# One joined first stage, and experts in 32-row blocks on four column groups with a fixed order of weights

## The chip, the cores and the metric

The kernel runs on one core of one Trainium2 chip. The metric is the device time of one execution in microseconds (us). The core has five engines with a queue of instructions each: TensorE (PE) for products and transposes, VectorE (DVE), ScalarE (ACT), GpSimd (POOL) and SyncE (SP). They meet through semaphores. SP, POOL and ACT issue transfers, which 16 DMA engines carry out.

## The reference, cut to what matters

Two streams, 256 context rows and 1024 latent rows of D = 1024, pass a convolution layer and a gated linear attention (GLA) layer. Each layer is followed by a mixture of 32 experts, in which every row goes to two experts of one group. All data are float32. The first layer works on all 1280 rows, the second one on the 1024 latent rows.

```python
x = x + sincos_2d(...)                         # latent rows only
h = modulate(rmsnorm(x, g), shift, scale)      # h * (1 + scale) + shift, from silu(c) @ ada_w + ada_b
a, g = split(h @ pw1_w + pw1_b); u = depthwise_conv31(a * sigmoid(g))   # then layernorm, silu, pw2
# experts: top-1 of 4 groups, top-2 of its 8 experts; for each pair of row and expert e
y = (silu(h @ w1[e]) * (h @ w3[e])) @ w2[e]    # 1024 -> 512 -> 1024, weighted sum of two
```

With the reference's inputs the router gives each expert of layer 0 between 1 and 14 blocks of 32 rows, 96 in all (42 blocks of 128 rows); in the fixed order of the change they are 1, 2, 1, 12, 1, 1, 1, 8, 3, 1, 1, 6, 1, 2, 1, 8, 2, 1, 1, 11, 4, 1, 1, 2, 1, 1, 1, 3, 1, 1, 1, 14. Layer 1 has 79 blocks of 32 rows (32 of 128): one expert with 1, sixteen with 2, fourteen with 3, one with 4. Every expert has at least one block, used or not.

## The kernel before, in words

The program is a row of stages with a barrier between them. Tiles have 128 rows: 2 of context, 8 of latent rows.

`modulation` computes the shift and scale rows of layer 0 (4 loads of 2 MB of `ada_w`, `ada_acc`) and adds the position to the latent rows on DVE (L191). `normalise` loads the rows back, scales them (L295, L298), transposes them on TensorE into `norm_pt` and writes the high part (ACT, L263) and the low part (DVE, L302) of the transposed rows, `ht_conv_hi` and `ht_conv_lo`. `conv_taps` then loads the first columns of the weights, splits them too (L516, L555), and computes product, gate (L563) and the 31 taps, channels of 128 at a time; the taps run on DVE. Next to it, modulation rows of later stages are computed as units of four column groups of TensorE (L488, `taps_ada_acc`).

The function `product3` (L97 to L101) is the float32 product of the expert stage: with each operand split in a high and a low part it issues three fast products, high by high (L99), low by high (L100), high by low (L101).

`route` plans a layer's blocks: DVE picks the experts and counts ranks, two small products give sums, DVE builds two tables, and 20 products `route_pi` (L1048) turn them into the list of rows of each block, `plan_token`. `plan_block` holds each block's expert, `plan_fresh` whether it is a new one.

`experts` walks over blocks of 128 rows in a loop whose body holds two blocks. SP reads the block's expert from `plan_block` and, where it is fresh, loads three matrices of 2 MB as six halves of 1 MB (`moe_w_raw`, L1282), each once the raw buffer has been split. ACT makes the high parts (L1408), DVE the low ones (L1479). POOL gathers the block's rows (`moe_xg`), TensorE transposes them (L1349), multiplies with the pair w1 and w3 (`moe_pg`, `moe_pu`), transposes the product (`moe_pat`, L1388) and multiplies with w2 (`moe_py`) one block late. ACT stores the result (`scratch_experts_out`). A block takes 24 calls of `product3`, that is 72 products of 128x512: 16 calls for the pair, 8 for w2. The later stages `combine_values` and `combine` gather the results by `plan_slot`.

## Time and the profile before

| what | value |
|---|---|
| median of 3 runs | 3072.42 us (3071.2 to 3075.68) |
| profiled execution | 3072.33 us, span 3070.6 us |
| mean granted clock | 0.899 |
| PE, DVE, ACT, POOL busy | 82%, 65%, 47%, 11% of the span |
| DMA | 689.13 MB, 224 GB/s over the span |

The stages by their first instruction: modulation from 0 us, `normalise` 66, `conv_taps` 120.9, `conv_out` 545, `route` 737.8, `experts` 781, `combine_values` 1577, GLA 1848, second `route` 2330, second `experts` 2370, `combine` 2985 to 3070.6. A time in the rows below is one of that span; the share of an engine over the span is a mean over stages with different limits.

### The profile page before, as it was taken

How to read it: one execution, taken by the hardware profiler on the slowest of the kernel's cores; microseconds unless marked ns; L12 is line 12 of the kernel's file. 1: busy time of each engine (PE TensorE's matmuls, PEld its weight loads, DVE VectorE, ACT ScalarE, POOL GpSimd, SP SyncE). 2: the span in 40 equal slices, each digit the busy share in tenths (PEclk: the TensorE clock that was granted, in tenths of full speed). 3: DMA queues.
4: the chain of work that ended last, by engine and by line, in shares of the span. 5: the costliest groups of instructions: out<-in, count | busy, mean ns of one | idle time of the engine just before them, and what ended most of it. 6: DMA issues, size and time to landing. Idle time of an engine off the chain costs nothing. (4 is left out here: it accounts for less than half of the span.)

```text
span 3070.6 us, 40694 instructions
## 1 busy us (share of the span) xinstructions
PE 2519.3 (82%) x13249; PEld 2033.0 (66%) x13249; DVE 2006.1 (65%) x1989; ACT 1432.9 (47%) x1596; POOL 331.4 (11%) x381
## 2 busy tenths in 40 slices
PE   4488773695799999999948998979693999999970
PEld 0467662584588888888836876768583788888850
DVE  1559999665657786588526402347565788888855
ACT  0311001452546676577424313458331777777742
POOL 0000000100001000100012100043100100010004
PEclk8589887797799999999978999989796999999985
DMA  9354341221878899799655411025551999999956
GB/s 306 119 166 140 127 159 70 99 103 65 291 261 306 323 331 357 264 360 389 247 182 202 143 52 46 14 78 171 205 191 61 375 389 385 389 388 394 394 211 227
DMA packets 294341, 689.13 MB, mean 224 GB/s; under 512 B 22764, under 2 KB 49588, under 8 KB 294222
## 3 DMA queue, kind: packets, MB, share of 16 engines
q1 hardware_dynamic: 263058, 584.81, 52.8%
q0 software_dynamic: 17472, 56.72, 5.6%
q10 hardware_dynamic: 13712, 46.30, 4.0%
q8 instruction: 61, 1.00, 0.1%
q14 instruction: 38, 0.31, 0.0%
HBM read 597.74 MB, written 91.06 MB: 224 GB/s over the span
## 5 line engine op out<-in xcount | busy, mean ns | idle before, releaser
L1479 DVE TENSOR_TENSOR moe_w_lo<-moe_w_raw,moe_w_hi 128x2048 fp32r<-128x2048 f32 x384 | 861.8, 2285 | 81.8 <-ACT moe_w_hi L1408 48.0
L1408 ACT ACTIVATE moe_w_hi<-moe_w_raw 128x2048 fp32r<-128x2048 f32 x384 | 713.8, 1908 | 59.1 <-issue 38.3
L99 PE MATMUL moe_pg<-moe_w_hi,moe_xt_hi 128*128 128x512 f32 x592 | 243.4, 411 | 11.3 <-DVE moe_xt_lo L1490 5.9
L99 PE MATMUL moe_py<-moe_w_hi,moe_at_hi 128*128 128x512 f32 x592 | 242.0, 409 | 11.9 <-DVE moe_w_lo L1479 8.2
L100 PE MATMUL moe_pg<-moe_w_lo,moe_xt_hi 128*128 128x512 f32 x592 | 236.6, 400 | 0.0
L101 PE MATMUL moe_pg<-moe_w_hi,moe_xt_lo 128*128 128x512 f32 x592 | 236.1, 399 | 0.0
L100 PE MATMUL moe_py<-moe_w_lo,moe_at_hi 128*128 128x512 f32 x592 | 235.4, 398 | 0.0
L101 PE MATMUL moe_py<-moe_w_hi,moe_at_lo 128*128 128x512 f32 x592 | 235.3, 397 | 0.0
L101 PE MATMUL moe_pu<-moe_w_hi,moe_xt_lo 128*128 128x512 f32 x592 | 234.3, 396 | 0.0
L99 PE MATMUL moe_pu<-moe_w_hi,moe_xt_hi 128*128 128x512 f32 x592 | 234.1, 396 | 0.0
L100 PE MATMUL moe_pu<-moe_w_lo,moe_xt_hi 128*128 128x512 f32 x592 | 234.1, 396 | 0.0
L1525 DVE TENSOR_TENSOR moe_a<-moe_sil,moe_pu 128x512 f32<-128x512 f32 x74 | 50.9, 688 | 182.0 <-issue 133.2
L531 ACT ACTIVATE taps_sg<-taps_zg,channel_vectors 128x512 f32<-128x512 f32 (+1 forms) x24 | 14.8, 616 | 285.5 <-PE taps_za L101 285.5
L1418 ACT ACTIVATE moe_y<-moe_py 128x1024 f32<-128x1024 f32 x74 | 76.0, 1027 | 148.8 <-PE moe_py L101 148.8
L1433 ACT ACTIVATE moe_xt_hi<-moe_pxt 128x1024 fp32r<-128x1024 f32 x74 | 75.8, 1025 | 134.5 <-PE moe_pxt L1349 134.5
L99 PEld LDWEIGHTS moe_pg<-moe_w_hi,moe_xt_hi 128*128 128x128 f32 x592 | 113.1, 191 | 36.2 <-issue 12.4
L99 PEld LDWEIGHTS moe_py<-moe_w_hi,moe_at_hi 128*128 128x128 f32 x592 | 112.4, 190 | 35.9 <-issue 12.3
L1311 POOL COPY moe_idx<-plan_token 128x1 int32 (+1 forms) x76 | 16.0, 210 | 1077.1 <-PE moe_pxt L1349 1076.9
L101 PEld LDWEIGHTS moe_pg<-moe_w_hi,moe_xt_lo 128*128 128x128 f32 x592 | 113.0, 191 | 27.4
L101 PEld LDWEIGHTS moe_py<-moe_w_hi,moe_at_lo 128*128 128x128 f32 x592 | 112.2, 190 | 27.1
L99 PE MATMUL cv_acc<-cv_w_hi,ht_next_hi 128*128 128x512 f32 x288 | 116.9, 406 | 14.8 <-DVE ht_next_lo L2038 14.8
L99 PEld LDWEIGHTS moe_pu<-moe_w_hi,moe_xt_hi 128*128 128x128 f32 x592 | 111.2, 188 | 26.9
(348 smaller groups left out, 5397.5 us busy)
## 6 DMA issues: line engine op xcount, KB each, us to landing
moe_w_raw<-in_moe_w SPq DMA_DIRECT2D x384, 1024.0 KB, 12.7
taps_ada_w<-in_ada_w SPq DMA_DIRECT2D x40, 1024.0 KB, 6.9
scratch_experts_out<-moe_y ACTq DMA_DIRECT2D x57, 512.0 KB, 6.4
taps_raw<-in_conv_pw_w SPq DMA_DIRECT2D x20, 512.0 KB, 8.6
scan_v<-scratch_gla_values SPq DMA_DIRECT2D x20, 512.0 KB, 3.6
ada_w<-in_ada_w SPq DMA_DIRECT2D x4, 2048.0 KB, 29.8
cv_raw<-in_gla_w_in SPq DMA_DIRECT2D x16, 512.0 KB, 4.8
scratch_gla_out<-scan_o SPq DMA_DIRECT2D x16, 512.0 KB, 6.4
```

The lines of the kernel that those rows point to most:

```text
L99: pe.matmul(out, xh, wh, start=start, stop=False)
L100: pe.matmul(out, xh, wl, start=False, stop=False)
L101: return pe.matmul(out, xl, wh, start=False, stop=stop)
L531: act.activation(sg[g][:, 0:m], zg[g][:, 0:m], ACT.Sigmoid, bias=vecs[:, n, V_BG:V_BG + 1])\
L1311: pool.tensor_copy(idx[:, :], plan.token[:, ds(k, 1)]).then_inc(s("idx_ready"), 1)
L1408: act.activation(hi[m][:, cut, :], raw[m][p][:, cut, :], ACT.Copy).then_inc(s(f"{m}_hi{h}"), 1)
L1418: act.activation(y[:, :], py[:, :], ACT.Copy).then_inc(s("y_out"), 1)
L1433: act.activation(xt_hi[:, :, :], pxt[:, :, :], ACT.Copy).then_inc(s("xt_hi"), 1)
L1479: dve.tensor_tensor(lo[m][:, cut, :], raw[m][p][:, cut, :], hi[m][:, cut, :].bitcast(F32), ALU.subtract).then_inc(s(f"{m}_lo{h}"), 1)
L1525: dve.tensor_tensor(a[:, :], sil[:, :], pu[:, :], ALU.mult).then_inc(s("a_ready"), 1)
```

## The change

It has three parts.

1. `modulation` and `normalise` become one stage, `front`. POOL loads the rows into eight buffers; the position's row half comes from a product on TensorE (`front_pp`); ACT scales the rows by their norm, TensorE transposes them at once, and DVE copies them unmodulated into `taps_out` (`vt`). The shift and scale rows are computed as four units of four column groups, transposed, and become columns (`mod`). `conv_taps` starts by modulating the transposed rows with these columns and splitting them. The first two pieces of its weights are loaded by `front`, its small rows too. The zeros that the expert stage wrote for unused blocks (`moe_zero`) are written once, by one transfer from ACT in `conv_taps`.
2. `route` plans blocks of 32 rows. Numbers of blocks come from three operations that round (`whole`). The table of a block's expert is gone; `plan_ends` says at which block each expert ends. `route_pi` works in four column groups. The comparing row of numbers is loaded a stage earlier (`ranks`). SP issues the weights of the first three experts at once.
3. `experts` takes the experts in a fixed order, `EXPERT_ORDER`, through four buffers of 6.29 MB (`Feed`). SP loads expert x + 3 when TensorE is through with x - 1. There is no splitting: products are plain float32. A block has 32 rows and is computed in four column groups: 32 products of 32x256 for the pair (each column group another quarter of the columns), 2 transposes of x, 16 products for w2, 1 transpose. Rows come as 128 quarters of 1 KB, by gathers issued four blocks ahead. TensorE's program holds, for each expert of a body of four, four straight copies of a block's instructions and two more inside loops; a copy has some 200 instructions, TensorE's program grows from 59 to 134.6 stretches of 256 instructions.

Its core:

```diff
-GROUPS, PER_GROUP, EXPERTS, FF, BLK = 4, 8, 32, 512, 128
+GROUPS, PER_GROUP, EXPERTS, FF, BLK = 4, 8, 32, 512, 32
+EXPERT_ORDER = [g * PER_GROUP + e for e in range(PER_GROUP) for g in range(GROUPS)]
...
+                        act.activation(ht.hi[:, k, t0:t0 + m], vt[:, k, t0:t0 + m], ACT.Copy).then_inc(s("ht_hi"), 1)
...
+                def modulate(g, k):
+                    t0, m, _ = CONV_GROUPS[g]
+                    st = CTX if g == 0 else LAT
+                    dve.tensor_scalar(vt[:, k, t0:t0 + m], vt[:, k, t0:t0 + m], mod[:, SC1, st, k:k + 1],
+                                      mod[:, SH1, st, k:k + 1], ALU.mult, ALU.add).then_inc(s("modulated"), 1)
+                def row_low(g, k):
+                    t0, m, _ = CONV_GROUPS[g]
+                    dve.wait_ge(s("ht_hi"), g * KC + k + 1)
+                    dve.tensor_tensor(ht.lo[:, k, t0:t0 + m], vt[:, k, t0:t0 + m], ht.hi[:, k, t0:t0 + m].bitcast(F32),
+                                      ALU.subtract).then_inc(s("ht_lo"), 1)
+                order = [(g, k) for g in range(len(CONV_GROUPS)) for k in range(KC)]
+                LAG = 3
+                for i in range(len(order) + LAG):
+                    if i < len(order):
+                        modulate(*order[i])
+                    if i >= LAG:
...
+    BUFS, AHEAD = 4, 3
+    PAIR = 2 * KC * FF
+    WORDS = PAIR + FF // P * D
...
+    def load_pair(self, sp, x):
+        e, b = EXPERT_ORDER[x], x % self.BUFS
+        for m, src in enumerate((self.d.w1, self.d.w3)):
+            for h in range(2):
+                sp.dma_start(self.pair[:, b, m, h * KC // 2:(h + 1) * KC // 2, :].rearrange("p (s c) n -> p s (c n)", c=2),
+                             src[self.layer, e, h * D // 2:(h + 1) * D // 2, :].rearrange("(s p c) n -> p s (c n)", p=P, c=2))\
+                    .then_inc(self.sem(f"pair_loaded{b}"), 16)
+    def load_back(self, sp, x):
+        e, b = EXPERT_ORDER[x], x % self.BUFS
+        for h in range(2):
+            sp.dma_start(self.back[:, b, 2 * h:2 * h + 2, :],
+                         self.d.w2[self.layer, e, h * FF // 2:(h + 1) * FF // 2, :].rearrange("(k p) n -> p k n", p=P))\
+                .then_inc(self.sem(f"back_loaded{b}"), 16)
...
+def route(nc, d, layer, streams, plan, lg, ranks, feed):
...
-        in_blk = ph.sb("in_blk", [P, 2 * nt, nb + 1])
...
+                for x in range(feed.AHEAD):
+                    feed.load_pair(sp, x)
+                    feed.load_back(sp, x)
...
+                    if j % nt == 0:
+                        pe.wait_ge(s("hot_slots"), 2 * (j // nt + 1))
+                    for r in range(0, P, BLK):
+                        last = pe.matmul(pi[r:r + BLK, :], in_slot[:, j, :], in_blk[:, j, :],
+                                         start=j == 0, stop=j == 2 * nt - 1)
                 last.then_inc(s("slots_done"), 1)
...
+                def whole(out, values, shift, floor):
+                    link(dve.tensor_scalar(out, values, 1.0 / BLK, shift, ALU.mult, ALU.add))
+                    link(dve.tensor_scalar(out, out, ROUND, None, ALU.add))
+                    link(dve.tensor_scalar(out, out, ROUND, floor, ALU.subtract, ALU.max))
...
+                whole(over, mine, -(BLK - 1) / (2 * BLK), 0.0)
+                link(dve.tensor_tensor(first, first, over, ALU.add))
+                link(dve.scalar_tensor_tensor(mine, over, -float(BLK), mine, ALU.mult, ALU.add))
...
+                for x in range(EXPERTS):
+                    times = x // BUFS + 1
+                    sp.wait_ge(feed.sem(f"pair_loaded{x % BUFS}"), 64 * times)
+                    sp.sem_inc(s("pair_ready"), 1)
+                    sp.wait_ge(feed.sem(f"back_loaded{x % BUFS}"), 32 * times)
+                    sp.sem_inc(s("back_ready"), 1)
+                    if 1 <= x < EXPERTS - feed.AHEAD:
+                        done = sp.value_load(plan.ends[0:1, x - 1:x], min_val=1, max_val=nb)
+                        sp.wait_ge(s("pair_done"), done)
+                        feed.load_pair(sp, x + feed.AHEAD)
+                        sp.wait_ge(s("back_done"), done)
+                        feed.load_back(sp, x + feed.AHEAD)
...
+                    pool.tensor_copy(idx[:, p:p + 1], plan.token[:, ds(k, 1)]).then_inc(s("idx_ready"), 1)
+                    pool.wait_ge(s("idx_ready"), k + 1)
                     pool.sem_inc(s("gathers"), 1)
...
+                    pool.indirect_dma_start(xg[p][:, :], None, cut_rows, bass.IndirectOffsetOnAxis(idx[:, p:p + 1], 0))\
+                        .then_inc(s(f"gathered{p}"), 16)
...
+                def out_product(out, buf):
+                    for c in range(STRIPS):
+                        for j in range(STRIPS):
+                            last = pe.matmul(out[j * BLK:(j + 1) * BLK, 0:CUT], at[:, c * BLK:(c + 1) * BLK],
+                                             feed.back[:, buf, c, j * CUT:(j + 1) * CUT], start=c == 0, stop=c == STRIPS - 1)
+                    last.then_inc(s("back_done"), 1)
+                def rows_of(k, x, b, nth):
+                    pe.wait_ge(s("xt_ready"), k + 1)
+                    if nth == 0:
+                        pe.wait_ge(s("pair_ready"), x + 1)
+                    for c in range(KC):
+                        for j in range(STRIPS):
+                            last = pe.matmul(pg[j * BLK:(j + 1) * BLK, 0:2 * P].rearrange("t (m n) -> t m n", m=2),
+                                             xt[:, c % 2, (c // 2) * BLK:(c // 2 + 1) * BLK],
+                                             feed.pair[:, b, :, c, j * P:(j + 1) * P], start=c == 0, stop=c == KC - 1)
+                    last.then_inc(s("pair_done"), 1)
+                    turn_x(k + 1)
+                    if started(k, 1):
+                        pe.wait_ge(s("at_ready"), k)
+                        if nth < 2:
+                            pe.wait_ge(s("back_ready"), x + nth)
+                        pe.wait_ge(s("y_out"), k)
+                        out_product(py, (b - 1) % BUFS if nth == 0 else b)
+                    pe.wait_ge(s("a_ready"), k + 1)
+                    pe.transpose(pat[:, 0:P], a[:, :], ident[:, :]).then_inc(s("at_turned"), 1)
+                def expert(x, b):
+                    first = 0 if isinstance(x, int) and x == 0 else \
+                        pe.value_load(plan.ends[0:1, ds(x - 1, 1)], min_val=1, max_val=nb)
+                    end = pe.value_load(plan.ends[0:1, ds(x, 1)], min_val=1, max_val=nb)
+                    rows_of(first, x, b, 0)
+                    for r in range(1, SOME):
+                        with pe.If(first + r < end):
+                            rows_of(first + r, x, b, r)
+                    with pe.If(first + SOME < end):
+                        with pe.Fori(SOME, MANY) as r:
+                            with pe.If(first + r < end):
+                                rows_of(first + r, x, b, SOME)
+                        with pe.If(first + MANY < end):
+                            with pe.Fori(MANY, (nb - EXPERTS) // 2) as r:
+                                with pe.If(first + r < end):
+                                    rows_of(first + r, x, b, SOME)
+                SOME, MANY = 4, 16
                 pe.wait_ge(s("ident"), 16)
-                turn_x(1)
-                blocks(pe, body, lambda count, last: out_product(count, last, 1))
+                turn_x(0)
+                for b in range(BUFS):
+                    expert(b, b)
+                with pe.Fori(1, EXPERTS // BUFS) as i:
+                    for b in range(BUFS):
+                        expert(i * BUFS + b, b)
+                count = pe.value_load(plan.block[0:1, 0:1], min_val=plan.fewest, max_val=nb)
+                pe.wait_ge(s("at_ready"), count)
+                pe.wait_ge(s("back_ready"), EXPERTS)
+                out_product(py_last, (EXPERTS - 1) % BUFS)
             @block.scalar
             def _(act):
                 act.preload_act_table(ACT.Silu)
```

TensorE's queue in the expert stage before: the end of one block, the branch to the loop's next block, and the start of its products.

```order
L99 MATMUL moe_py<-moe_w_hi,moe_at_hi 128x512
L100 MATMUL moe_py<-moe_w_lo,moe_at_hi 128x512
L101 MATMUL moe_py<-moe_w_hi,moe_at_lo 128x512
L1388 MATMUL moe_pat<-moe_ident,moe_a 128x128 x4
L1225 UNCONDITIONAL_BRANCH
L1225 ISA
L1228 COMPARE_AND_BRANCH
L1371 REGISTER_ALU
L99 MATMUL moe_pg<-moe_w_hi,moe_xt_hi 128x512
```

In the changed kernel TensorE has this between two experts: two values are read, then comes the first block of the expert and, behind a branch, the next.

```order
L1382 TENSOR_LOAD plan_ends
L1382 ISA x2
L1383 TENSOR_LOAD plan_ends
L1383 ISA x2
L1359 REGISTER_ALU
L1364 MATMUL moe_pg<-feed_w,moe_xt 32x256 x32
L1344 REGISTER_ALU
L1346 MATMUL moe_pxt<-moe_ident,moe_x_rows 128x128 x2
L1352 MATMUL moe_py<-feed_w,moe_at 32x256 x16
L1377 MATMUL moe_pat<-moe_ident,moe_a 128x128
L1386 COMPARE_AND_BRANCH
L1364 MATMUL moe_pg<-feed_w,moe_xt 32x256 x32
```

What one block does is now 51 calls, and each copy stands behind its own branch; an expert with fewer blocks than copies jumps over the rest.

SP's queue from the end of the planning on, before: the last constant of `route`, the barrier (L1031, L1263), and then weights whose expert is read from the plan.

```order
L1036 DMA route_next_e<-const_next_expert 1x32
L1031 UNCONDITIONAL_BRANCH
L1263 UNCONDITIONAL_BRANCH
L1265 DMA moe_ident<-const_ident 128x128
L1222 TENSOR_LOAD plan_block
L1222 ISA x2
L1277 TENSOR_LOAD plan_block
L1277 ISA x2
L1282 ISA
L1282 DMA moe_w_raw<-in_moe_w 128x4x512
L1282 ISA
L1282 DMA moe_w_raw<-in_moe_w 128x4x512 x3
```

In the changed kernel three experts (L1023 the pair, L1030 w2), of which the last two are shown, stand ahead of the barrier, the fourth behind it; the read of the plan only says when a buffer is free.

```order
L1023 DMA feed_w<-in_moe_w 128x2x1024 x4
L1030 DMA feed_w<-in_moe_w 128x2x1024 x2
L1023 DMA feed_w<-in_moe_w 128x2x1024 x4
L1030 DMA feed_w<-in_moe_w 128x2x1024 x2
L1091 UNCONDITIONAL_BRANCH
L1296 UNCONDITIONAL_BRANCH
L1298 DMA moe_ident<-const_ident 128x128
L1023 DMA feed_w<-in_moe_w 128x2x1024 x4
L1030 DMA feed_w<-in_moe_w 128x2x1024 x2
L1310 TENSOR_LOAD plan_ends
L1310 ISA x2
```

The weights moved from behind the plan to ahead of it.

DVE's queue in the first stages, before: the position of the last of eight tiles, then the two modulation rows, and in `normalise` two passes of a whole tile; the third one (L302) follows a tile later.

```order
L191 TENSOR_TENSOR ada_xin<-ada_xin,ada_pos_col 128x512
L196 TENSOR_TENSOR ada_row<-ada_acc,ada_bias 2x1024 x2
L129 UNCONDITIONAL_BRANCH
L343 UNCONDITIONAL_BRANCH
L277 MEMSET norm_eps 128x1
L282 SCALAR_TENSOR_TENSOR norm_scale<-norm_scale,norm_gain 128x1024
L308 UNCONDITIONAL_BRANCH
L288 RECIPROCAL norm_stat<-norm_stat 128x1
L295 SCALAR_TENSOR_TENSOR norm_h<-norm_x,norm_stat,norm_scale 128x1024
L298 TENSOR_TENSOR norm_h<-norm_h,norm_shift 128x1024
```

In the changed kernel the queue of `front` has one copy a tile, and modulating and splitting follow in `conv_taps`.

```order
L327 COPY taps_out<-front_pt 128x8x128
L323 RECIPROCAL front_stat<-front_stat 128x1
L327 COPY taps_out<-front_pt 128x8x128 x2
L343 COPY mod<-front_pp 128x8 x4
L349 SCALAR_TENSOR_TENSOR mod<-mod,front_gain 128x8 x2
L159 UNCONDITIONAL_BRANCH
L537 UNCONDITIONAL_BRANCH
L539 MEMSET taps_ada_acc 128x512
L540 TENSOR_TENSOR taps_both<-channel_vectors 128x8x15
L542 COPY taps_both<-channel_vectors 128x8
L607 TENSOR_SCALAR taps_out<-taps_out,mod 128x256 x4
L613 TENSOR_TENSOR ht_conv_lo<-taps_out,ht_conv_hi 128x256
```

The passes of a tile no longer wait for the modulation rows; the 24 pairs of L607 and L613 stand behind them.

## Rows read from the trace of the kernel before

**Rows 1.** Windows, one per stage: busy us (instructions), granted clock, DMA share, GB/s.

```profile
core 0: us, PE busy (x) PEld busy (x) DVE busy (x) ACT busy (x) POOL busy (x), PEclk, DMA share, GB/s
0.00:120.90 120.90, 53.05 (x144) 21.56 (x144) 52.54 (x62) 26.56 (x44) 0.22 (x5) 0.71 0.70 233
120.90:168.80 47.90, 32.03 (x181) 27.60 (x184) 5.42 (x7) 5.12 (x6) 2.38 (x3) 0.77 0.29 93
...
737.80:781.00 43.20, 11.25 (x44) 9.78 (x44) 32.61 (x85) 1.73 (x4) 0.01 (x1) 0.50 0.02 5
781.00:1577.00 796.00, 767.90 (x3536) 624.76 (x3536) 529.69 (x318) 487.50 (x361) 72.98 (x88) 0.98 0.84 307
...
2370.00:2985.00 615.00, 587.97 (x2696) 478.07 (x2696) 506.03 (x288) 450.50 (x320) 60.06 (x65) 0.97 0.99 367
```

**Rows 2.** Timeline of the first stages: start, duration, engine, line, operation.

```profile
1.70 11.11 SPq L137 DMA_DIRECT2D ada_w<-in_ada_w  x3
...
61.45 2.34 DVE L196 TENSOR_TENSOR ada_row<-ada_acc,ada_bias 2x1024 f32<-2x1024 f32 x2
...
118.98 1.22 DVE L302 TENSOR_TENSOR ht_conv_lo<-norm_pt,ht_conv_hi 128x1024 fp32r<-128x1024 f32 x1 [1.98 <-ACT ht_conv_hi L263]
...
168.82 1.15 DVE L563 SCALAR_TENSOR_TENSOR taps_u<-taps_za,channel_vectors,taps_sg 128x512 f32<-128x512 f32 x1 [9.74 <-ACT taps_sg L531]
```

**Rows 3.** Timeline of the planning of layer 0 and the first product behind it.

```profile
741.31 0.20 DVE L1071 TENSOR_REDUCE route_gm<-scores 128x10 f32<-128x40 f32 x1 [4.44 <-DMA route_next_e<-const_next_expert]
...
770.80 8.78 PE L1048 MATMUL route_pi<-route_in_blk,route_in_slot 128*128 128x53 f32 x40 [18.08 <-DVE route_in_blk L1148]
...
783.52 18.09 SPq L1282 DMA_DIRECT2D moe_w_raw<-in_moe_w  x9
...
797.52 0.77 PE L99 MATMUL moe_pg<-moe_w_hi,moe_xt_hi 128*128 128x512 f32 x1 [2.69 <-issue]
```

**Rows 4.** Page, costliest groups of instructions: count, busy us, mean ns.

```profile
L1479 DVE TENSOR_TENSOR moe_w_lo<-moe_w_raw,moe_w_hi 128x2048 fp32r<-128x2048 f32 x384 | 861.8, 2285 | 81.8 <-ACT moe_w_hi L1408 48.0
...
L99 PE MATMUL moe_pg<-moe_w_hi,moe_xt_hi 128*128 128x512 f32 x592 | 243.4, 411 | 11.3 <-DVE moe_xt_lo L1490 5.9
...
L99 PEld LDWEIGHTS moe_pg<-moe_w_hi,moe_xt_hi 128*128 128x128 f32 x592 | 113.1, 191 | 36.2 <-issue 12.4
```

**Rows 5.** Timeline of TensorE around a modulation unit, and inside a block.

```profile
247.55 0.39 PE L101 MATMUL taps_za<-ht_conv_hi,taps_w_lo 128*128 128x512 f32 x1
247.87 0.40 PE L481 MATMUL taps_ada_acc<-taps_ada_b,taps_one 1*2 1x128 f32 x8
248.20 1.93 PE L488 MATMUL taps_ada_acc<-taps_ada_w,silu_c 128*2 128x128 f32 x64
250.05 0.50 PE L99 MATMUL taps_zg<-ht_conv_hi,taps_w_hi 128*128 128x512 f32 x1
...
2505.90 0.40 PE L101 MATMUL moe_pu<-moe_w_hi,moe_xt_lo 128*128 128x512 f32 x1
2506.13 1.04 PE L1349 MATMUL moe_pxt<-moe_ident,moe_xg 128*128 128x128 f32 x8
2506.92 0.48 PE L99 MATMUL moe_py<-moe_w_hi,moe_at_hi 128*128 128x512 f32 x1
```

**Rows 6.** Windows inside the two expert stages, columns as in the first group.

```profile
2400.00:2960.00 560.00, 557.16 (x2579) 454.09 (x2580) 489.35 (x279) 430.74 (x307) 57.26 (x62) 1.00 1.02 382
1000.00:1500.00 500.00, 500.00 (x2323) 407.54 (x2322) 376.15 (x224) 340.97 (x249) 47.75 (x55) 1.00 0.92 337
```

**Rows 7.** DMA queues (packets, MB, share) in 2400:2960, and the gathers of the run.

```profile
q1 hardware_dynamic: 80250, 190.94, 91.1%
...
moe_xg<-scratch_experts_in,moe_idx POOLq DMA_INDIRECT x76, 7.6
```

**Rows 8.** DMA queues in 121:546: the instructions' own queue.

```profile
q8 instruction: 20, 0.33, 0.3%
```

**Rows 9.** Instructions of tile taps_acc: count, duration min/median/max.

```profile
L573 DVE TENSOR_SCALAR taps_acc<-taps_u,taps_both x8: 550/554/574, 170.9 to 504.6; 128x649 f32<-128x649 f32 x8
```

More of the change, by code:

```diff
@@ L1019, in route @@
[L1019 to L1026 removed]
+        sb = feed.room()
+        before = sb([P, P])
+        ones = sb([P, P])
+        iota = sb([P, P])
@@ L1027, in route @@
+        mine = sb([P, 2, nt])
+        first = sb([P, 2, nt])
+        over = sb([P, 2, nt])
+        need = sb([P, EXPERTS])
+        ends = [sb([P, EXPERTS]) for j in range(2)]
+        in_slot = sb([P, 2 * nt, BLK])
+        in_blk = sb([P, 2 * nt, nb + AHEAD_X])
         pr = ph.ps("pr", [P, nt * EXPERTS])
         pa = ph.ps("pa", [P, nt * EXPERTS])
-        pi = ph.ps("pi", [P, nb + 1])
+        pi = ph.ps("pi", [P, nb + AHEAD_X])
         with nc.Block() as block:
@@ L1213, in experts @@
-        pu = ph.ps("pu", [P, FF])
-        pat = ph.ps("pat", [P, FC, P])
-        py = ph.ps("py", [P, D])
-        def blocks(eng, body, tail=None, otherwise=None):
-            count = eng.value_load(plan.block[0:1, nb:nb + 1], min_val=plan.fewest, max_val=nb)
-            for k in range(2):
-                body(k, k)
-            with eng.Fori(1, nb // 2) as i:
-                for p in range(2):
-                    k = i * 2 + p
+        ident = ph.sb("ident", [P, P])
+        idx = ph.sb("idx", [P, UNROLL], I32)
@@ L1228, in blocks @@
+        cut_rows = d.hd.rearrange("t (s n) -> (t s) n", n=CUT)
+        def blocks(eng, body, tail=None):
+            count = eng.value_load(plan.block[0:1, 0:1], min_val=plan.fewest, max_val=nb)
+            for k in range(UNROLL):
+                body(k, 0, k)
+            with eng.Fori(1, nb // UNROLL) as i:
+                for p in range(UNROLL):
+                    k = i * UNROLL + p
                     with eng.If(k < count):
-                        body(k, 2, i, p)
-                    if otherwise:
-                        with eng.If(k >= count):
-                            otherwise(k)
+                        body(k, i, p)
@@ L1397, in _ @@
                 act.preload_act_table(ACT.Silu)
-                def high(m, n, before, least, p=0, loads=None):
-                    for h in range(2):
-                        cut = slice(h * half[m], (h + 1) * half[m])
-                        act.wait_ge(s(f"{m}_raw{h}{p}"), (n if loads is None else loads) * 16)
-                        if h == 0 and least:
-                            act.wait_ge(s(f"{m}_done"), before)
-                        act.activation(hi[m][:, cut, :], raw[m][p][:, cut, :], ACT.Copy).then_inc(s(f"{m}_hi{h}"), 1)
```

958 lines of the change are left out of this document (417 added, 541 removed).

## The prediction

> **What bounds the kernel now.** I read the windows by stage first: in the two expert stages TensorE is busy for 767.90 of 796.00 us and for 587.97 of 615.00, at a granted clock near 1, and DMA for 0.84 and 0.99 of the time [rows 1]. Inside them both limits are closer still: from 2400 to 2960 TensorE is busy for 557.16 of 560 us while DMA moves 382 GB/s at a share of 1.02, and from 1000 to 1500 it is never idle at 337 GB/s [rows 6]. So layer 0 is bound by TensorE, and layer 1 by TensorE with DMA hardly behind it. A change that takes work from TensorE in layer 1 meets DMA at once. The casts (861.8 us of DVE [rows 4]) lie beside TensorE and are worth nothing by themselves.
>
> The group rows give 592 first products, 8 for each of 74 blocks of 128 [rows 4]. Products of 512 columns start 0.23 us apart (2505.90 to 2506.13), eight transposes take 0.79 us to the next start, 0.1 each [rows 5]. A block of 128 is thus 72 x 0.231 = 16.6 us and about 2 us of transposes and changes, 19 us, whether it is full or not.
>
> Second, the timeline of the start: the last modulation row is made at 61.45 + 2.34, the last low part at 118.98 + 1.22, and DVE's third gate, behind which the taps run without a break, is at 168.82 [rows 2]. The stages up to there are a chain of DMA, DVE and TensorE, each waiting on the one before; granted clock 0.71 and 0.77 [rows 1]. Third, the planning: DVE begins at 741.31, 3.4 us after the stage, when a constant has landed; `route_pi` runs from 770.80 to 779.6; weights are asked for at 783.52 and the first product is at 797.52 [rows 3].
>
> **The first stages, -66 us.** The passes of normalise (118.98 + 1.22 - 66.4 = 54 us behind the rows that need modulation) no longer wait for modulation. What `front` must move is 8.4 MB of `ada_w`, 5.2 MB of rows in and 4.2 MB of latent rows out, 2.1 MB of early weights and small rows, about 20.5 MB in all; at 337 GB/s [rows 6] it takes 61 us, and with a start of some 3 us behind the first small loads I take its end as 64. DVE has one copy and two half-tile additions a tile and ends with the transfers. Then `conv_taps` has 24 passes of L607 (8 of 256 columns, 16 of 512; 649 columns take 0.55 us [rows 9], so 0.3 and 0.45) and 24 subtractions of up to 0.7 us, 10 + 14 us, and one split of weights, 2.3 us [rows 4]. The high parts lie on ACT beside it. Behind the last low part stand 24 products at 0.23 us, a sigmoid and the gate of 1.15 us: third gate at 64 + 26 + 12 = 102 instead of 168.8, -66. The bounds: -75 (transfers at 382 GB/s and the products right behind the splits), -55 (transfers in a tail of small rows, TensorE at half clock). The taps behind it are DVE's and stay as they are; the zeros are one transfer of 4 MB where 0.3 to 0.4 of DMA is used, hidden; if it weren't, it would cost 12 us.
>
> **The two plans, -11 us.** Each loses the wait for the constant, 3.4 us [rows 3], the comparing of numbers (about 1 us) and gets narrower tables (1.1 us): 5.5 us. The operations on `plan_block` lie beside `route_pi` today and give nothing. `route_pi` is issued four times as often at a quarter of the rows; rounds of four go in parallel in the unit's rows (below), so the 8.78 us stay. Bounds: -2 and -8 each.
>
> **A block of 32 rows, 6.5 us.** No row shows a 32x256 product. The nearest is the modulation unit: 64 records in column groups of 128 columns take 250.05 - 248.20 = 1.85 us, with the change out of it 1.74, or 0.109 us for a round of four; one product is two records [rows 5]. So four groups do run at once, and a round of four products of 256 columns is 2 x 0.215 us. A block has 8 rounds for the pair and 4 for w2: 12 x 2 x 0.215 = 5.16 us, 3 transposes 0.33, and five changes between products in groups and whole ones, which cost 0.1 us (247.55 + 0.23 to 247.87) to 0.2 us each, 1.0 us. 6.5 us. Lower bound 5.7 (changes free). Upper bound 8: loading 128 columns of the other operand takes 0.191 us [rows 4], 32 of them a quarter; if it doesn't hide, 24 rounds lose 0.05 to 0.06 us each. The small operations of DVE and ACT are under 2.5 us a block and hide behind TensorE's 6.5; the gather lands in 7.6 us [rows 7] and has four blocks, 26 us, for it. The Trainium skill ("TensorEngine Tiling (Array Packing)", "Key Properties") says that a change of the tiling mode drains TensorE; the rows agree that it costs something, and the price is theirs.
>
> **The jumps, 1 us each.** A block has about 200 instructions, and an expert with one block jumps over three copies and the loops, one with two over two; all others leave or enter a loop once. With the counts given that is 74 jumps in layer 0 and 50 in layer 1. Before, the body of two blocks is jumped back in once for 38 us of work, and TensorE was not idle at all from 1000 to 1500 [rows 6], so a far branch inside a long queue of work is hidden there. Now one comes each 6.5 to 13 us, with new code behind it. 20 packets of code take 0.3% of 16 engines in 424 us, 1.0 us each [rows 8]; that is my price, between 0 (fetched ahead, or behind the queue of instructions) and 3 (two packets in a row, behind the weights). Even the gather's 7.6 us [rows 7] is no bound that these rows exclude. The Trainium skill speaks against the change here ("Runtime: NRT & Kernel Launch", "Instruction fetch mechanics"): a taken branch whose target is not in the current window waits for the fetch of that page. By that rule the jumps cost at least one fetch each; by the idle-free window of before they would cost nothing.
>
> **The weights.** An expert is 6.29 MB, at 385 GB/s 16.3 us (bounds 365 and 400), and each block adds 0.26 MB of gather and store, 0.7 us. Three experts are asked for at the start of the plan, some 34 us before its end; the fourth when the plan ends, x + 3 when x - 1 is through. I walked through the experts in order with these prices.
>
> *Layer 0:* 96 x 6.5 = 624, 74 jumps 74, start 10 (gather 7.6 and a turn), end 4. The four loaded experts carry TensorE over the short ones until late; the last load ends 651 us after the plan, since buffers are held during the blocks of the experts with 12, 8 and 11, and the last five experts wait for it 34 us altogether; the 14 blocks of the last stand behind it. Sum 746 for 796, -50.
>
> *Layer 1:* 79 x 6.5 = 514, jumps 50, start 10, end 4, waits 4: 582 for 615, -33. Loads alone end at 543, and the last expert's 4 blocks, 26 us, behind them: 573, so both limits are within 9 us.
>
> **Sum:** 3072.3 - 66 - 11 - 50 - 33 = 2912 us, for the profiled execution, which is 0.1 us from the median of the runs.
>
> **The rivals.**
> 1. *Jumps are hidden and changes are cheap* (5.7 to 6.5 us a block, no price for a jump). For it: no idle time at the loop's branch before [rows 6]. Then DMA is the bound of both stages: 671 to 710 and 570 to 577 us, total 2825 to 2871; with 400 GB/s 2786. Chance 0.22.
> 2. *A jump costs 2 us.* 124 jumps cost 124 us more, of which waits for weights give back 32: 792 and 628, total 3004. Chance 0.13.
> 3. *The other side: a jump costs 3 us or more.* Place: between the experts, PE waiting for its own instructions. 222 + 150 us of jumps, no waits for weights any more: 860 + 678, total 3122, slower. It decides from 2.6 us a jump. For it: DMA is nearly full with weights just when the code must come, and the gather takes 7.6 us in that state; against it: 1.0 us a packet [rows 8] and no stall of before. Chance 0.08. At 5 us it would be 3370.
> 4. *Blocks are slow,* 8 us, for the loads of operands show in each round: 871 + 696, total 3151. Chance 0.05; against it the unit's 0.109 us.
> 5. *The clock isn't granted,* since TensorE has gaps: at the lower level a block takes 11.6 us, total 3766. The granted clock is 0.5 where TensorE works in pieces, in the plan [rows 1], 1.00 where it is never idle [rows 6]. 0.02.
> 6. *The front doesn't shorten,* because the transfers stay the bound up to 100 us: 2912 + 35 = 2947, inside the forecast's own range.
>
> **How the numbers follow.** The forecast has 0.50, with a range of its own of 2871 to 2989 (7 us a block at its upper end, 50 to 77 us more in the sum). With rival 1 at 0.22, 2 at 0.13, 3 at 0.08, 4 at 0.05 and 5 at 0.02 all is given out. The range reaches down to 2790, the whole of rival 1 but its edge, and up to 3070, with rival 2; outside are 3, 4, 5, 0.15, and little below. 0.2%, 6 us, is about what a measurement can tell from no change. Faster are the forecast, 1 and 2, less 0.02 for a case that falls within 0.2%: 0.83; within it 0.02; slower 3, 4 and 5: 0.15.
>
> **What the profile after would show.** Front: third gate near 102 us, DMA over 300 GB/s up to 64. Plan: first operation of DVE at its start, first product some 10 us behind its end. Block: starts of one block's first product to the next 6.5 us apart inside the 12 to 14 blocks of a long expert, at clock 1; twice that if rival 5 holds. Jump: the space between the last product of a one-block expert and the first of the next, over that of blocks in a straight row; over 2.6 us rival 3 is right. Weights: TensorE's waits for `pair_ready` at the last five experts of layer 0, about 34 us, and DMA near 385 GB/s throughout layer 1. The prediction is wrong if a block costs under 5.7 or over 7.5 us, if the loads run under 350 GB/s because their 4 KB pieces or the gathers of 1 KB slow them, or if TensorE stands for its code.

## The result: 20% slower

The changed kernel takes 3697.11 us (median of 4 runs, 3691.89 to 3700.29), the one before 3071.81 in the same series; the ratio is 1.203 (1.201 to 1.205). The forecast was 2912 us with a range of 2790 to 3070. The page of the profiled execution:

```profile
span 3697.4 us, 61615 instructions
...
PE 2376.5 (64%) x24807; PEld 1567.7 (42%) x24808; DVE 1102.6 (30%) x1927; ACT 695.3 (19%) x1470; POOL 418.7 (11%) x610
...
q8 instruction: 388, 6.36, 0.8%
...
L1364 PE MATMUL moe_pg<-feed_w,moe_xt 128*32 128x256 f32 x11200 | 788.7, 439 | 804.0 <-issue 803.0
```

TensorE is busy for 2376.5 us, 143 less than before, but before the products of a pair (w1 and w3) it is idle for 804.0 us, 803.0 of them behind "issue": the engine waited for nothing that the profile shows. The queue that carries instructions (q8) has 388 packets. The windows by stage, with the columns of [rows 1]: the front; the plan and the experts of layer 0; the experts of layer 1.

```profile
0.00:75.80 75.80, 43.11 (x397) 25.98 (x398) 24.91 (x46) 29.50 (x48) 10.13 (x25) 0.86 0.77 271
...
687.40:724.50 37.10, 8.67 (x164) 7.12 (x164) 24.30 (x78) 1.75 (x4) 0.00 (x0) 0.59 0.94 369
724.50:1850.00 1125.50, 667.13 (x9506) 347.18 (x9506) 83.90 (x289) 101.87 (x290) 115.94 (x200) 0.78 0.51 192
...
2640.00:3607.00 967.00, 563.52 (x7823) 293.69 (x7823) 69.05 (x238) 84.13 (x239) 96.22 (x166) 0.78 0.59 221
```

In the expert stages nothing is full: TensorE 59 and 58%, DMA 0.51 and 0.59, DVE 7%; the granted clock fell from 0.98 and 0.97 to 0.78. A stage is measured here from its first record to the first record of the next one. So taken, the expert stage of layer 0 has 1130.5 us (724.5 to 1855.0) in place of 798.0 (781.0 to 1579.0), +333, and that of layer 1 has 973.8 (2644.1 to 3617.9) in place of 623.3 (2367.9 to 2991.1), +350. The start is 50 us shorter, the plan of layer 0 6 us; the plan of layer 1 and `combine` are as long as before. Together that is +627, the span's difference.

The timeline of TensorE at the first experts of layer 0 (1, 2 and 1 blocks) shows where the time lies. One product is two records.

```profile
742.65 6.02 PE L1364 MATMUL moe_pg<-feed_w,moe_xt 128*32 128x256 f32 x64 [0.47 <-ACT moe_xt L1417]
748.60 0.51 PE L1346 MATMUL moe_pxt<-moe_ident,moe_x_rows 128*128 128x128 f32 x2
749.40 0.33 PE L1377 MATMUL moe_pat<-moe_ident,moe_a 128*128 128x128 f32 x1 [0.29 <-DVE moe_a L1464]
768.65 4.98 PE L1364 MATMUL moe_pg<-feed_w,moe_xt 128*32 128x256 f32 x64 [18.93 <-issue]
773.56 0.50 PE L1346 MATMUL moe_pxt<-moe_ident,moe_x_rows 128*128 128x128 f32 x2
773.99 1.93 PE L1352 MATMUL moe_py<-feed_w,moe_at 128*32 128x256 f32 x32
775.86 0.33 PE L1377 MATMUL moe_pat<-moe_ident,moe_a 128*128 128x128 f32 x1
776.11 3.66 PE L1364 MATMUL moe_pg<-feed_w,moe_xt 128*32 128x256 f32 x64
...
792.64 4.93 PE L1364 MATMUL moe_pg<-feed_w,moe_xt 128*32 128x256 f32 x64 [10.31 <-issue]
```

The reader is to see two things. A block is quick: the 64 records of a pair take 3.66 us at full clock, a whole block 6.15. And between two experts TensorE stands, here for 18.93 and 10.31 us; the products behind these pauses take 4.9 to 5 us, at a granted clock of 0.72 and 0.73. Over the run there are 62 pauses of more than 3 us, up to 19.8, 779 us in all; the pairs behind them take 4.9 to 9.5 us in place of 3.66, 169 us more in all, of which 24 are stops of up to 3.1 us inside the pair and the rest is the lower clock. The records of TensorE's sequencer in the same trace (it executes branches and register loads, which the views leave out) name the wait. Start, us, kind, line:

```
749.39  0.37 COMPARE_BRANCH L1386      copy 2 jumped over
749.90  5.70 COMPARE_BRANCH L1386      copy 3
755.66  5.69 COMPARE_BRANCH L1386      copy 4
761.41  5.66 COMPARE_BRANCH L1388      both loops, 400 instructions
767.12  0.32 TENSOR_LOAD    L1382      the next expert begins
```

And the DMA queues over that stretch of 19 us, with over 370 GB/s in its first 16:

```profile
q1 hardware_dynamic: 1758, 6.74, 89.0%
q0 software_dynamic: 48, 0.13, 1.8%
q8 instruction: 3, 0.05, 1.1%
```

Three branches, three packets of code. Over the run TensorE's branches take 737 us; 123 of them, over 1 us each, take 681, 5.5 on average. Most experts with one block show one pattern: about 0.35 us at the second copy, 3.0 to 3.6 at the third, 5.2 to 6.2 (or 0.23) at the fourth, 5.5 to 7.8 at the loops. The first expert, shown above, has 5.7 at the third; at the end of layer 0, where no weights are loaded any more, 3.0 to 4.3 are left. Inside the loop of a long expert (12 blocks) a return costs 0.22.

The theory for the experiments: **TensorE waits for its own code when a jump leads to instructions that are not on hand,** 5.5 us a time in place of the 1.0 forecast, and the six copies of a block per expert make the jumps. Rivals: each taken branch costs so much whatever its distance; the wait is one for SP or the weights in disguise; bytes are the real limit and the pauses hide it. "Far jump" stands below for a branch of over 1 us.

### The profile page after: what moved, and what is told of

It is laid out like the page before. It is cut to its first block and busy times, and to the rows that moved or that the text cites. A ratio compares the mean times of both kernels' runs of the same rounds, so it can differ in the third digit from the quotient of the medians.

```text
span 3697.4 us, 61615 instructions
## 1 busy us (share of the span) xinstructions
PE 2376.5 (64%) x24807; PEld 1567.7 (42%) x24808; DVE 1102.6 (30%) x1927; ACT 695.3 (19%) x1470; POOL 418.7 (11%) x610
## 5 line engine op out<-in xcount | busy, mean ns | idle before, releaser
L1364 PE MATMUL moe_pg<-feed_w,moe_xt 128*32 128x256 f32 x11200 | 788.7, 439 | 804.0 <-issue 803.0
L1364 PEld LDWEIGHTS moe_pg<-feed_w,moe_xt 128*32 128x32 f32 x11200 | 397.5, 126 | 1136.2 <-issue 965.7
L1352 PE MATMUL moe_py<-feed_w,moe_at 128*32 128x256 f32 x5536 | 334.6, 382 | 0.0
L1352 PEld LDWEIGHTS moe_py<-feed_w,moe_at 128*32 128x32 f32 x5536 | 161.5, 109 | 110.7
L1323 POOL DMA_INDIRECT moe_xg<-scratch_experts_in,moe_idx x183 | 178.7, 977 | 144.0 <-POOL moe_idx L1320 144.0
L105 PE MATMUL cv_acc<-cv_w_hi,ht_next_lo 128*128 128x512 f32 x288 | 115.2, 400 | 0.0
L104 PE MATMUL cv_acc<-cv_w_lo,ht_next_hi 128*128 128x512 f32 x288 | 114.7, 398 | 0.0
L579 DVE SCALAR_TENSOR_TENSOR taps_acc<-taps_back,channel_vectors,taps_acc 128x649 f32<-128x649 f32 x120 | 107.0, 892 | 0.0
L567 DVE SCALAR_TENSOR_TENSOR taps_acc<-taps_u,taps_both,taps_acc 128x649 f32<-128x649 f32 x120 | 107.0, 891 | 0.0
L594 DVE SCALAR_TENSOR_TENSOR taps_acc<-taps_ahead,channel_vectors,taps_acc 128x649 f32<-128x649 f32 x112 | 92.0, 892 | 0.0
L1417 ACT ACTIVATE moe_xt<-moe_pxt 128x256 f32<-128x256 f32 x177 | 67.8, 383 | 55.6 <-PE moe_pxt L1346 34.8
```

The costliest lines, as they stand in the source:

```text
L104: pe.matmul(out, xh, wl, start=False, stop=False)
L105: return pe.matmul(out, xl, wh, start=False, stop=stop)
L567: dve.scalar_tensor_tensor(acc[0][:, :], src, tap, acc[0][:, :], ALU.mult, ALU.add)\
L579: dve.scalar_tensor_tensor(acc[1][:, :], src, tap, acc[1][:, :], ALU.mult, ALU.add)\
L594: dve.scalar_tensor_tensor(acc[q][:, :], src, tap, acc[q][:, :], ALU.mult, ALU.add)\
L1323: pool.indirect_dma_start(xg[p][:, :], None, cut_rows, bass.IndirectOffsetOnAxis(idx[:, p:p + 1], 0))\
```

## The experiments

Times are medians; a ratio is one to the kernel before in the same series. e1 and e3 are single runs with outputs that are not the reference's: the second router sees other values, so layer 1 has 80 blocks in place of 79, spread otherwise over the experts. A line of waits has the total in us, how many there were and the longest.

**e1: the changed kernel without loads behind the fourth expert.**

```diff
-                    if 1 <= x < EXPERTS - feed.AHEAD:
-                        done = sp.value_load(plan.ends[0:1, x - 1:x], min_val=1, max_val=nb)
-                        sp.wait_ge(s("pair_done"), done)
-                        feed.load_pair(sp, x + feed.AHEAD)
...
```

> The changed kernel, but SP loads only the first four experts of each layer; all later blocks use the weights that lie in the four buffers, so the output is not the reference's. In the trace of the changed kernel TensorE's branches take 710 us (123 over 1 us, most 5.5 to 7.5 us, and 3.0 to 4.3 us at the end of layer 0, where the loads are over). Theory code fetch, slowed by the weights: without loads a long branch takes about 3 us, TensorE's branches together 300 to 400 us, and the execution 3697 - 350 = about 3350 us. Rival, code fetch with a price of its own that does not depend on the load: the branches stay at 5.7 us and the time within 30 us of 3697. Rival, the weights are the true limit and the branches only hide it: the two expert stages fall to blocks alone, 96 x 6.15 = 590 and 79 x 6.15 = 486 us, total about 2690.

Measured 3416.54 us. TensorE's branches take 492 us, 121 of them over 1 us: nearly as many far jumps, and each costs 3.6 us on average in place of 5.5. So neither rival holds: the price falls by a third without the loads, and with no weights to wait for 3417 us remain. The estimate of about 3 us a jump was too low.

The records of the code packets split the price. Where one packet falls into a far jump (81 of them in the changed kernel, 74 here), it starts 3.1 us behind the branch in the changed kernel and 0.6 us behind it here, takes 1.0 and 1.1 us, and TensorE goes on 1.4 us after its end in both (medians). The loads thus add to the time before the packet starts, and hardly to the packet. The line of TensorE's waits:

```profile
PE moe_pg L1358 <- issue: 523.7, 70, 14.2
```

**e2: two copies in place of six.**

```diff
-                    for r in range(1, SOME):
-                        with pe.If(first + r < end):
-                            rows_of(first + r, x, b, r)
-                    with pe.If(first + SOME < end):
-                        with pe.Fori(SOME, MANY) as r:
...
+                    with pe.If(first + 1 < end):
+                        with pe.Fori(first + 1, end) as k:
+                            rows_of(k, x, b, 1)
```

> The changed kernel, but TensorE's program for an expert has two copies of a block in place of six: the first block straight, then one loop from the second block to the expert's last, so that an expert with one block jumps over 200 instructions once and no other jumps forward at all. Everything else is the same. Theory code fetch: skips of 200 instructions took 0.36 us where the one before was not jumped, so nearly all of the 710 us go, but for 7 returns of the outer loop a layer at 7.3 us (102 us); weights then limit parts of both stages: layer 0 some 715 us in place of 1130, layer 1 some 590 in place of 977, total 2895, between 2830 and 2980. Rival, each taken branch of TensorE costs 5.7 us whatever its distance (a drained engine, not its code): 19 one-block experts, 14 returns and some 110 loop turns pay it, about 800 us, total 3600 to 3800. Rival, TensorE's four groups slow each other once they are not interrupted: blocks of more than 7 us, total over 3000.

Measured 3000.46 us, ratio 0.976 (0.974 to 0.978): 697 us less than the changed kernel, with the same operations on every engine. All branches take 34.8 us, two are over 1 us (3.8 and 3.6, both at code of the outer loop that is reached for the first time), and the instructions' queue has 86 packets for 388. The returns of the outer loop, over some 1,650 instructions, take 0.2 us, not the 7.3 that I had expected. "Any taken branch costs 5.7 us" is dead: 94 branches take 0.2 us each, jumps over a copy of 200 instructions among them. TensorE's waits now:

```profile
PE moe_pg L1364 <- SPq L1305: 173.6, 32, 12.2
...
PE moe_pxt L1346 <- DMA moe_ident<-const_ident: 49.1, 2, 26.7
...
PE moe_pg L1364 <- issue: 13.5, 18, 3.8
```

The branch's 803 us are 13.5, and a new wait has come up, for SP's word that a pair of weights is there. It is a part of why e2 misses its 2830 to 2980: e11 below puts 57 us on it.

**e3: e2 without the loads.**

> The loops of e2 with the loads of e1 (only the first four experts of each layer; the output is not the reference's). What is left is TensorE's own time. Theory code fetch: 96 x 6.15 + 7 returns at 3 us + start 17 + end 6 = 635 us for layer 0, 79 x 6.15 + 21 + 23 = 530 for layer 1, total 3697 - 1130 - 977 + 635 + 530 = 2755. If it is within 20 us of e2, weights do not limit e2; by the walk they should, by 100 us or more. Rival (each taken branch has its price): as e2, over 3500.

Measured 2780.51 us, 26 over the estimate and 220 less than e2. So weights, or SP's word on them, limit e2; without either, the changed kernel with two copies needs about 2781 us. The run takes both away and doesn't tell them apart.

**e4: the front alone.** The new first stage and tap stage, with plan and experts as before.

> The joined first stage and the start of the tap stage as changed, with planning and experts as before (blocks of 128, split products, the zeros written for unused blocks). In the changed kernel the third gate is at 118.4 us in place of 168.8. Theory: the gain of the front is kept whole to the end, since DVE's taps behind it run without a break and no stage overlaps another: 3072 - 50 = 3022 us, between 3015 and 3027. Rival: part is lost again, since the rest of the tap stage was covered by something else (units of modulation, weights); then the gain is under 40 us.

Measured 3023.89 us, ratio 0.984 (0.982 to 0.985): 51 us of 3075.22, kept whole. The third gate in its timeline, 51 us earlier than the 168.82 of before:

```profile
117.81 1.15 DVE L547 SCALAR_TENSOR_TENSOR taps_u<-taps_za,channel_vectors,taps_sg 128x512 f32<-128x512 f32 x1 [9.74 <-ACT taps_sg L518]
```

**e5 and e6: an earlier start.** e5 loads the identity ahead of the weights; e6 also asks for only two experts ahead of the barrier.

```diff
+                sp.dma_start(feed.ident[:, :], d.ident).then_inc(feed.sem("ident"), 16)
-                for x in range(feed.AHEAD):
+                for x in range(feed.EARLY):
                     feed.load_pair(sp, x)
```

> e2 (3000.5 us), but the identity matrix that TensorE's transposes need is loaded by SP in the planning ahead of the weights, not behind them. In e2 the first transpose of the expert stage waits for it, 16 to 18 us behind the stage's start in both layers, while the gather had landed 10 us earlier. Theory: layer 0 starts some 10 us earlier and keeps it, since the loads of the later experts are asked for that much earlier too; layer 1 is bound by the weights and keeps 0 to 5. Total 2985 to 2990. Rival: both stages are bound by the bytes, the earlier start turns into a longer wait for weights, time within 4 us of e2.

> e5, and only two experts are asked for ahead of the barrier, the third and fourth behind it. In the changed kernel DVE ends the plan at 719.6 us and the stage ends at 724.5, since SP was still handing over the third expert's transfers until 723.6. Theory: the barrier moves 4 to 5 us ahead in each layer and the transfers go on without a gap, since 12.6 MB take 33 us: 8 us less than e5, of which layer 1 may give back some. Rival: the queue runs dry around the barrier, no gain or a loss of some us.

Measured 2998.86 and 2998.26 us, ratios 0.976 and 0.976: nothing, both expectations missed, and e5's rival has the number (within 4 us of e2). In layer 0 it does not have the reason. In e6 the barrier is 4 us earlier (720.3 for 724.5) and the first rows are turned at 728.70, and still the first product stands at 741.43:

```profile
724.24 9.09 SPq L1024 DMA_DIRECT2D feed_w<-in_moe_w  x4
...
733.36 7.87 SPq L1031 DMA_DIRECT2D feed_w<-in_moe_w  x2
741.43 4.99 PE L1365 MATMUL moe_pg<-feed_w,moe_xt 128*32 128x256 f32 x64 [12.06 <-SPq L1306]
```

SP hands over six transfers of the fourth expert. Five of them take it 2.3 to 5.5 us each, where the first transfers of the plan took 0.4 to 0.9; presumably it has to wait for room in its queue. Only when it is through with the last, at 741.2, does it report the first expert's weights, which were asked for some 50 us earlier.

**e7: three copies.** e2 with the second block straight as well.

> e2 with a third copy of a block in TensorE's program for each expert (first block straight, second straight behind a branch, the rest in the loop). The jump of an expert with one block goes over 400 instructions in place of 200, and the body of the outer loop grows from some 1,650 to 2,450 instructions. The work is the same. Theory (code that isn't on hand costs a fetch; a short skip and a body of 1,650 are on hand): the jumps over 400 cost 3 to 7 us for 20 one-block experts, the 14 returns of the outer loop 7 us each if the body no longer fits; TensorE's branches take 100 to 230 us in place of 35; half or more of it hides behind waits for weights, time 3020 to 3100. If the returns stay at 0.2 us, the body still fits and only the skips count, branches 70 to 130 us. Rival (distance doesn't matter): as e2, 3000.

Measured 3091.94 us, ratio 1.005 (1.004 to 1.007), 91 us over e2. Branches take 220 us, 185 more than in e2, so that about half of it hides behind other waits. All 12 returns of the outer loop take 6.1 to 7.4 us each, and 30 skips 1.4 to 6.8. So a body of some 1,650 instructions is on hand when the loop returns, one of some 2,450 is not. It is not the distance of a jump that is paid: a skip of 200 instructions costs 0.2 us in e2 once its code has been there, and up to 5.6 in e7. What is paid is code that isn't on hand.

**e8: weights in pieces of 2 KB.** e6 with the pair read in rows of 2 KB.

> e6 with the pair's weights read in pieces of 2 KB as before, in place of 4 KB, and the halves of a quarter row taken in their plain order to match. In e2 4 KB pieces move at 22.8 bytes per ns and engine, 354 GB/s from 2350 to 2850, against 382 GB/s in the kernel before with mostly 2 KB pieces. Theory A: the size of the pieces is not what holds the rate (gathers and stores of quarter rows are), time within 6 us of e6. Theory B: 4 KB pieces are worse with the small ones between them; 2 KB pieces bring 375 GB/s, layer 1 some 30 us shorter. Theory C: 4 KB pieces are better, and 2 KB ones cost 10 to 40 us.

Measured 3047.02 us, ratio 0.991 (0.990 to 0.993), 49 us more than e6: theory C's way, a little over its range. But the rate between 2350 and 2850 is nearly the same, 356 GB/s for 354, at a share of 0.99 for 0.97, with half as many packets again for the same bytes. The 49 us stand in TensorE's waits for SP's word, first e6, then e8:

```profile
PE moe_pg L1365 <- SPq L1306: 206.3, 33, 18.2
PE moe_pg L1365 <- SPq L1306: 257.9, 40, 23.4
```

SP is held up longer in handing over (the longest tenth of its weight transfers take 5.4 us or more, in e6 3.5 or more) and reports later; the first product of layer 0 stands at 747.3 for 741.4. So the run doesn't show what the size of pieces costs where TensorE waits for the landing itself.

**e9: TensorE waits for the landing itself.** On top of e6.

```diff
-                    sp.wait_ge(feed.sem(f"pair_loaded{x % BUFS}"), 64 * times)
-                    sp.sem_inc(s("pair_ready"), 1)
...
+                    pe.wait_ge(feed.sem(f"{kind}_loaded{b}"), (i + 1) * (64 if kind == "pair" else 32))
```

> e6 (2998.3 us), but TensorE waits for the landing of the weights itself; SP no longer reports them between its own transfers. In e6 TensorE waits 206 us for SP's report of a pair, and SP's queue shows why: at 2464.87, 2482.73 and 2499.80 the report takes 0.02 us, right behind a transfer that SP was 2.4 to 3.3 us in handing over, so the weights had landed before; the first product of layer 0 is at 741.4 though its rows were ready at 729.8. Theory: reports come up to one hand-over late, 10 to 18 us; without them layer 0 starts at 731, and each wait is only for bytes. DMA is at a share of 0.97 in layer 1, so there only the lead of some 10 us is won; layer 0, with gaps in the transfers, wins 15 to 30. Total 2955 to 2975. Rival: bytes are the limit everywhere, and SP's report was never more than a few us late: 2990 to 2998, TensorE's waits move from SP to DMA.

Measured 2932.09 us, ratio 0.955 (0.953 to 0.956): 66 us less than e6, more than the 23 to 43 expected. The rival, 2990 or more, is dead. The first product stands at 728.3 in place of 741.4, and the last one of layer 0 at 1414 for 1463. TensorE's waits and the window inside layer 1 (columns of [rows 6]):

```profile
PE moe_pg L1363 <- DMA feed_w<-in_moe_w: 140.9, 25, 13.3
PE moe_pg L1363 <- issue: 24.5, 32, 4.0
PE moe_pxt L1341 <- DVE moe_x_rows L1448: 18.3, 2, 9.4
```

```profile
2280.00:2780.00 500.00, 413.50 (x6184) 227.55 (x6176) 54.54 (x187) 65.40 (x188) 71.97 (x125) 0.91 0.98 357
```

Now the wait is one for bytes: inside layer 1 DMA is at a share of 0.98 and 357 GB/s. This version takes 4.5% less than the kernel before and 21% less than the changed one.

**e10: that edit alone on the changed kernel.**

> The changed kernel (3697.1 us) with only that edit: TensorE waits for the landing of the weights itself, its program keeps six copies a block and expert. Theory code fetch: the weights are there long before TensorE has its code, so that the report costs next to nothing: 3685 to 3700, of which the earlier start may give 10. Rival: the 5.7 us at a branch are partly waits for SP in disguise; then the time falls by over 50 us.

Measured 3699.32 us, ratio 1.205 (1.203 to 1.207): nothing. Branches take 729 us, 120 of them over 1 us and 5.6 on average. With six copies TensorE comes too late for its weights anyway, so the price of a far jump is no wait for SP, and e9's gain exists only once these jumps are gone.

**e11: that edit alone on e2,** identity and third expert where the change has them.

> e2 (3000.5 us) with only the direct wait for the landing of the weights; the identity is again behind the weights, and three experts are asked for ahead of the barrier, as in the changed kernel. e5 and e6 gave nothing while SP's report came late. Theory (in a row: barrier, identity, report; the last one decides): now the first transpose waits for the identity until 741 again, in e9 it is at 727, and the gain of e9, 66 us, is kept but for 10 to 20 us in layer 0 and 5 to 10 in layer 1: 2945 to 2962. Rival: the early start is given back while waiting for bytes, and e11 equals e9 within 4 us (2928 to 2936).

Measured 2943.01 us, ratio 0.958 (0.956 to 0.959). Of e9's gain over e2, 68 us, the report is worth 57; identity and barrier, worth nothing in e5 and e6, are worth 11 behind it (9 by the ratios, whose intervals, 0.953 to 0.956 and 0.956 to 0.959, only just stay apart). e11 lies 2 us outside the 2945 to 2962 expected, and shows not the rival's equality.

## Why the prediction was wrong

**The step that failed is the price of a jump.** "20 packets of code take 0.3% of 16 engines in 424 us, 1.0 us each [rows 8]; that is my price". The packet does take 1.0 us (1.03 at 753.07 in the trace of after, 3.2 us behind the branch), but TensorE waits from its branch until the code can run: 5.70 us there, 3.2 before the packet starts and 1.5 behind its end; 5.5 on average over 123 branches. Their number was about right, 66 and 57 for 74 and 50 forecast. I had taken the time that a transfer occupies for the time that someone waits for it; the gather's row, 7.6 us from issue to landing [rows 7], was the right kind of number, and I named it and put it aside. Rival 3 had the place and the reason, with a chance of 0.08; its "At 5 us it would be 3370" was on the way. With 5.54 us a jump its sum is 3437; it left out the short branches (56 us) and what the pauses do to the products behind them, 169 us in 62 pairs, mostly by the lower clock. These three make 3662 of the 3697.

The rule of the Trainium skill ("Runtime: NRT & Kernel Launch", "Instruction fetch mechanics") that a taken branch to a page not in the window waits for its fetch was right, and I weighed it too lightly against "TensorE was not idle at all from 1000 to 1500 [rows 6]". The trace agrees with it, and e2 and e7 show why the row said nothing: before, the loop's body is some 350 instructions and returns into code that is on hand (0.22 us a return), and TensorE's longest branch of the whole run is 0.23 us.

**Point by point:**
- *Start, -66 us:* -50 (118.38 for 168.82 [rows 2]), e4 -51. Right in kind and kept whole. The term is off mainly in one place: `front` ends at 75.8, not 64. Its transfers did what was forecast, 313 GB/s up to 64, but the stage did not end with them:

```profile
0.00:64.00 64.00, 34.03 (x241) 19.75 (x242) 19.33 (x35) 26.33 (x41) 9.46 (x22) 0.87 0.89 313
64.00:75.80 11.80, 9.08 (x164) 6.23 (x156) 5.58 (x12) 3.17 (x7) 0.67 (x3) 0.79 0.12 46
```

  Behind 64 stands a chain that the forecast put at nothing: the last two modulation units (3.60 us at the lower clock, then 1.93), the last tiles, and the turning of the rows into columns. From the stage's end the third gate is 42.6 us away, 38 forecast. It lies 5 us outside the bound of -55.
- *Plans, -11 us:* -6 in layer 0 (37.1 for 43.1), nothing in layer 1 (37.2 for 37.3). DVE did better than forecast, 32.2 us in place of 42.3 and 28.5 in place of 36.4; but the stage can't end before SP has handed over the third expert's transfers, 4 us behind DVE in layer 0 and 8 in layer 1:

```profile
2635.09 0.27 DVE L1225 TENSOR_SCALAR plan_token<-feed_w 128x100 int32<-128x100 f32 x1
2638.25 4.91 SPq L1030 DMA_DIRECT2D feed_w<-in_moe_w  x2
...
2644.11 1.44 SPq L1298 DMA_DIRECT2D moe_ident<-const_ident  x1
```

- *A block, 6.5 us:* 6.15 at full clock. Right; no run shows the price of a change between groups and whole products by itself.
- *Weights:* 385 GB/s forecast, 354 to 357 inside layer 1 of e2 and e9, where it is the bound. The first bound of 365 was not low enough; 32 experts and 79 blocks are 222 MB, 624 us at 356 GB/s less the 34 us of lead. e9's layer 1 has 605 us from its first product to its last. The changed kernel itself, at 0.59 of DMA, never came to this bound.
- *SP's part:* not in the prediction. I had counted what SP issues, not what stands behind it: its reports and the end of the plan. The reports cost nothing in the changed kernel (e10) and 57 us as soon as the jumps were gone (e11).
- *Rival 5, the clock:* not as a state of its own; the granted clock fell to 0.78 behind the pauses, and came back to full inside long experts.

With the jumps repaired and the report direct, 2932 us stand against the 2912 forecast: errors of both signs (a longer front and slower bytes, quicker blocks and nearly free jumps) nearly cancel in it, so that the nearness proves no single term.

What stays open: what holds a packet of code back for 3.1 us while weights are loaded, and what the 1.4 us behind its end are. No kernel was made that changes only the other traffic's piece size at the jumps. Why a straight copy sometimes stops inside a pair, for up to 3.1 us, was not followed up either.

## What to carry to other kernels

Count the jumps into code that isn't on hand as you count products: here a skipped copy was paid at 3 to 8 us a jump, while a loop over some 1,650 instructions returned in 0.2. Here a loop with a trip count from a register beat straight copies under conditions by 697 us. An engine that issues transfers is a bad messenger, since its reports stand behind its hand-overs; let the consumer wait for the landing itself. And a wait hidden behind a larger one is worth nothing until that is gone: repair in the order in which they end last.

## What the runs showed of the hardware

- TensorE's wait at a jump to code that isn't on hand: 5.5 us on average while weights are loaded, 3.6 without (e1). Where one 16 KB packet of code falls into it, the packet starts after 3.1 us (0.6 without loads), takes about 1.0, and TensorE goes on 1.4 us after its end (medians).
- A loop body of about 1,650 instructions of TensorE returns in 0.2 us, one of about 2,450 in 6.1 to 7.4 (e2, e7). A skip of 200 instructions costs 0.2 us or several, by whether its code has been there (e2, e7). The other engines' branches in the changed kernel take under 0.08 us throughout.
- Float32 products of 32x256 in four column groups: the 32 products of a pair are 64 records in 3.66 us at full clock, four records every 0.215 us or so, and a whole block takes 6.15.
- Behind a pause at a jump TensorE's pair took 4.9 to 9.5 us, the next block's 3.66 again: short pauses cost twice.
- SP hands over a transfer of 1 MB in 0.4 to 0.9 us at the start of the plan, and five of the six of the fourth expert, behind eighteen others, in 2.3 to 5.5 (e6).
